# Two plain weight projections of the second block turned into products by blocks

## The chip, the cores and the metric

The kernel runs on one core of a Trainium2 chip, all in 32-bit floats. The metric is the device time of one launch in microseconds (us); three runs of the kernel before gave 4491.0 to 4492.48, with a median of 4491.58.

## The reference

The reference runs a sequence of 1024 tokens with a width of 1024 through two hybrid attention layers (the first block) and then one layer of the second block. Only the end of the second block matters here:

```python
mixed = (jax.nn.sigmoid(gate_a) * y_a + jax.nn.sigmoid(gate_b) * y_b) @ w_out[i]
x = layer_norm_2(DEEPNORM_ALPHA * x + mixed, ln1_g[i], ln1_b[i])

h = causal_dwconv(x @ w_up[i], conv_w[i], conv_b[i])
h_gate, h_val = jnp.split(h, 2, axis=-1)
ffn = (jax.nn.silu(h_gate) * h_val) @ w_down[i]
x = layer_norm_2(DEEPNORM_ALPHA * x + ffn, ln2_g[i], ln2_b[i])

ple = jax.nn.sigmoid(x @ w_ple_gate[i]) * (p[i] @ w_ple[i])
x = layer_norm_2(DEEPNORM_ALPHA * x + ple, ln3_g[i], ln3_b[i])
```

The change is to two 1024x1024 weight products, `@ w_out` (called out2 below) and `x @ w_ple_gate` (the ple gate).

## The kernel before, in words

The program writes one instruction stream for each engine by hand, and semaphores (`wait_ge`, `then_inc`) join them, so each engine runs its instructions in the order of its code and an instruction that waits holds up all that stand behind it. All on-chip data lies in one large tile called arena; all matmul results are in psum. A matmul of 32-bit floats is recorded as two passes on TensorE, and the trace's counts (x256) are counts of passes.

The second block ends in functions named `..._tail`, one for each engine: `pe_tail` (TensorE), `act_tail` (ScalarE), `dve_tail` (VectorE), and the streams of SP and GpSimd. The tokens are two halves of 512 columns (`HALF`), the width is eight tiles of 128 rows (`KD = 8`). On TensorE the order is: eight pairs of the mixing stage (L2773, `product`), out2 (L2739), the first units of the up projection taken plainly (L2727, `plain`), the remaining pairs of the up and down projections (L2773), the small product p @ w_ple (L2845), the ple gate (L2727), and the last normalisation.

A *pair* in this kernel is two output tiles by two runs of tokens that are worked out together by seven block products in place of eight (the scheme of Strassen and Winograd): four sums of weight blocks and four sums of data blocks are made first, and products 1, 6, 7, 4, 5, 2 and 3 are combined into the four output blocks. The mixing, up and down stages of the tail do this with products of 512 columns. The output projection of the first block does it too (`pe_outproj`, L1537), as a chain on 256 columns: each product is four matmuls with 256 columns, products 1, 6 and 7 are copied out of psum by ScalarE (L1675), VectorE adds the others to the copies (L1759), makes the sums of data (L1752) and also the sums of weights (L1741), and the next product of the chain accumulates in psum on top of the one that was copied. out2 and the ple gate are plain: for each half and each output tile, eight matmuls of 512 columns (16 passes).

Between the matmuls of a stage lie the layer normalisations (`layer`, `half`) of the stage before or of the first half of the same stage. Each is a sum of the eight tiles on VectorE (`summed`, L3001), a `mean` matmul (L2749), the subtraction on VectorE (`centre`, L3012), squares on ScalarE (`square`, L2871) that VectorE adds up (`squares`, L3018), a `variance` matmul (L2753), the inverse root on ScalarE (`root`: Ln at L2876 and Exp at L2878, each with a load of its function table), the multiplication by it on VectorE (`scale`, L3028), and gain and bias on ScalarE (`affine`, L2884). Three of them lie beside the two changed stages (`NORMED_IN`): normalisation (0, 0) in the second half of out2, (1, 1) in the first half of the ple gate and (2, 0) in the second. `SUB_SLOTS`, `SQUARE_SLOTS` and `SCALE_SLOTS` say behind which output tile i the centres and squares (i = 1, 2, 3) and the scales and affines (i = 5, 6, 7) stand. The mean of the next one, (0, 1) or (2, 1), follows the last tile.

Weights come as blocks of 512 KB in four buffers (`TAIL_W`), loaded by SP as soon as the block four places earlier is used up (`consumed`). GpSimd does nearly nothing in the tail.

## Time and profile before

| | before |
|---|---|
| median of 3 runs | 4491.58 us (4491.0 to 4492.48) |
| the profiled execution | 4496.65 us |
| its span on the core | 4494.5 us |
| TensorE busy | 4354.1 us, 97% of the span |
| VectorE busy | 2536.8 us, 56% |
| ScalarE busy | 1279.5 us, 28% |
| GpSimd busy | 56.0 us, 1% |
| mean granted clock of TensorE | 0.99 of full speed |
| DMA | 48 GB/s, mean over the span |

The span is what the profiler saw on the core; the time of the execution has 2.15 us around it. The profiled execution was 5.07 us slower than the median of the runs. In rows of the timeline, a number in square brackets is the time for which the engine stood idle before the row, and what it waited for.

### The profile page before, as it was taken

Reading aid. Unit: us, or ns where it says so; the run is one execution under the profiler, and the core shown is the slowest. Engines: PE = TensorE matmul, PEld = TensorE weight load, DVE = VectorE, ACT = ScalarE, POOL = GpSimd, SP = SyncE. Lnnn points to the kernel's source line nnn. Section 1 sums busy time; section 2 is a strip of 40 time slices with the busy share of each in tenths; the row PEclk is TensorE's granted clock in tenths of the full one; section 3 lists DMA queues with packets and bytes.
Section 4 is the critical chain, followed back from the end, with each engine's and each line's share of the span. In section 5 each row is a group of like instructions: output and inputs, shape, how many; then the busy total and the mean of one; then the engine's idle time right before and its main releaser. Section 6 shows DMA issues by size and latency. Waiting matters only on the chain.

```text
span 4494.5 us, 47632 instructions
## 1 busy us (share of the span) xinstructions
PE 4354.1 (97%) x19288; PEld 2491.4 (55%) x19288; DVE 2536.8 (56%) x4202; ACT 1279.5 (28%) x2050; POOL 56.0 (1%) x82
## 2 busy tenths in 40 slices
PE   7999999999998999999999999999999999999997
PEld 3554667886444678844467645555544444444443
DVE  7677556754586567528952314445443555556554
ACT  3004445522025455222023403333200311110024
POOL 1000000000000000000000000000000000000000
PEclk9999999999999999999999999999999999999999
DMA  7212000021120000200110020000122211111112
GB/s 289 75 61 89 1 1 1 2 107 61 47 94 19 1 1 2 84 28 29 38 38 28 20 75 19 20 19 10 38 75 70 69 40 47 47 38 66 47 47 75
DMA packets 50615, 215.57 MB, mean 48 GB/s; under 512 B 5024, under 2 KB 5024, under 8 KB 46816
## 3 DMA queue, kind: packets, MB, share of 16 engines
q1 hardware_dynamic: 36512, 142.62, 9.6%
q0 software_dynamic: 13888, 69.93, 4.1%
q8 instruction: 153, 2.51, 0.2%
q14 instruction: 62, 0.51, 0.0%
HBM read 189.46 MB, written 23.07 MB: 47 GB/s over the span
## 4 chain that ended last, share of the span: by engine, by line
PE 92%; DVE 4%; ACT 2%; DMA 1%; issue 1%; DVEq 0%; SPq 0%; ACTq 0%; POOL 0%; PEld 0%; PEldq 0%
PE psum L2773 21%; PE psum L709 9%; PE psum L1274 7%; PE psum L1312 5%; PE psum L1936 5%; PE psum L1293 5%; PE psum L1537 4%; PE psum L2390 4%; PE psum L399 3%; PE psum L2727 3%; PE psum L2049 3%; PE psum L2039 3%; PE psum L2412 2%; PE psum L2739 2%; PE psum L2076 2%; PE psum L2442 1%
## 5 line engine op out<-in xcount | busy, mean ns | idle before, releaser
L2773 PE MATMUL psum<-arena 128*128 128x512 f32 x2184 | 937.7, 592 | 0.9 <-DVEq L382 0.9
L2773 PEld LDWEIGHTS psum<-arena 128*128 128x128 f32 x2184 | 414.9, 190 | 523.0 <-issue 521.6
L3076 DVE TENSOR_TENSOR arena<-arena,psum 128x512 f32<-128x512 f32 x280 | 192.7, 688 | 405.9 <-PE psum L2773 397.4
L709 PE MATMUL psum<-arena 128*128 128x512 f32 x952 | 410.0, 592 | 0.0
L1274 PE MATMUL psum<-arena 64*128 64x256 f32 (+2 forms) x1584 | 381.9, 441 | 6.8 <-ACT arena L1227 5.8
L709 PEld LDWEIGHTS psum<-arena 128*128 128x128 f32 x952 | 180.9, 190 | 223.8 <-issue 222.4
L1293 PEld LDWEIGHTS psum<-arena 128*128 128x128 f32 x1968 | 229.4, 141 | 125.0 <-issue 102.3
L1347 ACT ACTIVATE arena<-psum,arena 128x1280 f32<-128x1280 f32 (+1 forms) x216 | 265.9, 1241 | 109.6 <-DVE arena L1378 104.6
L1293 PE MATMUL psum<-arena 128*128 128x128 f32 x1968 | 275.5, 275 | 10.8 <-DVE arena L1409 5.8
L1352 ACT ACTIVATE arena<-psum 128x512 f32<-128x512 f32 x294 | 164.8, 597 | 284.6 <-PE psum L1293 284.6
L1312 PE MATMUL psum<-arena 128*64 128x128 f32 x3936 | 238.7, 275 | 4.6 <-DVE arena L1394 2.8
L1312 PEld LDWEIGHTS psum<-arena 128*64 128x64 f32 x3936 | 212.9, 137 | 31.6 <-issue 16.6
L1537 PE MATMUL psum<-arena 128*128 128x256 f32 (+1 forms) x1120 | 222.6, 361 | 6.5 <-ACT arena L1675 4.2
L1936 PE MATMUL psum<-arena 128*128 128x512 f32 x512 | 226.1, 597 | 0.0
L1274 PEld LDWEIGHTS psum<-arena 64*128 64x128 f32 (+1 forms) x1584 | 192.0, 192 | 42.0 <-issue 25.0
L1537 PEld LDWEIGHTS psum<-arena 128*128 128x128 f32 x1120 | 196.7, 191 | 33.2 <-ACT arena L1675 5.4
L1378 DVE TENSOR_REDUCE arena<-psum 128x1 f32<-128x1280 f32 (+1 forms) x120 | 152.2, 1273 | 67.9 <-PE psum L1274 67.8
L2390 PE MATMUL psum<-arena 128*128 128x512 f32 x392 | 175.7, 600 | 0.0
L872 DVE SCALAR_TENSOR_TENSOR arena<-arena 128x1024 f32<-128x1024 f32 (+1 forms) x180 | 172.6, 1014 | 2.1
L2003 DVE TENSOR_SCALAR_CACHE_REDUCE arena<-arena 128x384 f32<-128x384 f32 (+2 forms) x192 | 168.9, 942 | 1.1
L805 DVE TENSOR_TENSOR arena<-arena,psum 128x512 f32<-128x512 f32 x119 | 81.8, 687 | 155.0 <-PE psum L709 145.5
L1394 DVE COPY arena<-psum 128x512 f32<-128x512 f32 x198 | 131.4, 685 | 67.0 <-PE psum L1293 63.6
(314 smaller groups left out, 5453.3 us busy)
## 6 DMA issues: line engine op xcount, KB each, us to landing
arena<-stream SPq DMA_DIRECT2D x228, 512.0 KB, 3.7
arena<-mod_t POOLq DMA_DIRECT2D x32, 512.0 KB, 4.7
arena<-mod_w POOLq DMA_DIRECT2D x4, 2048.0 KB, 16.3
gated<-arena POOLq DMA_DIRECT2D x8, 1024.0 KB, 4.7
arena<-stream SPq DMA_DIRECT2D x6, 1024.0 KB, 10.0
arena<-x SPq DMA_DIRECT2D x4, 1280.0 KB, 15.8
gated<-arena POOLq DMA_DIRECT2D x4, 1280.0 KB, 4.7
arena<-gated SPq DMA_DIRECT2D x1, 5120.0 KB, 15.7
```

What stands on the lines that cost most here:

```text
L709: last = nc.tensor.matmul(ps(PROJECT_BANKS[p], 512), lhsT=lhsT(k), rhs=rhs(k), start=k == 0, stop=k == 3)
L872: last = nc.vector.scalar_tensor_tensor(sb(acc, n), sb(u + i, n), par("dw", off=2 * i + j), sb(acc, n), ALU.mult, ALU.add)
L1274: last = nc.tensor.matmul(ps(score_at(steps[u], s) + c0, n), lhsT=q, rhs=keys, start=True, stop=True)
L1293: last = nc.tensor.transpose(ps(bank(steps[u], g) + i * P, P), sb(P_AT + s * TC + j * P, P), con("ident", P))
L1312: nc.tensor.matmul(ps(BANK7, P, 64 * s, 64 * s + 64), lhsT=sb(at + 64 * s, 64), rhs=sb(PT_AT + (s * nkt + j) * P, P), start=j == 0, stop=j ...
L1347: nc.scalar.activation(sb(P_AT + s * TC, n), ps(score_at(steps[u], s), n), ACT.Exp, bias=sb(MX_AT + s), accum_out=sb(SUM_AT + s)).then_inc ...
L1537: ins = nc.tensor.matmul(ps(out_bank(q, p), h), lhsT=lhsT(k), rhs=rhs(k), start=first and k == 0, stop=k == 3, skip_group_check=not first)
L1936: last = nc.tensor.matmul(ps((b % 2) * 1024 + c0, w), lhsT=sb(W_AT + (g % 2) * 1024 + k * P, P), rhs=x_rhs(k, c0, w), start=k == 0, stop=k ...
L2003: last = nc.vector.tensor_scalar(sb(RELU_AT + mask_at(j) - mask_at(2), w), sb(mask_at(j), w), sb(TRIAL + n), None, ALU.is_ge, ALU.add, acc ...
L2390: last = nc.tensor.matmul(ps(bank, HALF), lhsT=lhsT(k), rhs=rhs(k), start=k == 0, stop=k == 3)
L2773: last = nc.tensor.matmul(ps(pair_bank(j, p), HALF), lhsT=lhsT(k), rhs=rhs(k), start=k == 0, stop=k == nk - 1)
L3076: step(nc.vector.tensor_tensor(out, a, b, op), ev)
```

## The change

out2 and the ple gate are each computed by one chain of seven-product pairs (`chain(0)` and `chain(CHAIN)`). A pair q is two output tiles by one half of the tokens, split into two runs of 256 columns; each chain has eight of them, q = 0 to 7 and q = 8 to 15, the first four for the first half of the tokens. A product is four matmuls of 256 columns, so eight passes. Products 1, 6, 7 and 4 of a pair accumulate in the same bank (`run_bank`), and ScalarE copies the bank out (`copy`) between them, in the same way as in the first block. TensorE's order within a pair is six, five, seven, one of the next pair, four, two of the next pair, three.

The four sums of weights of each pair, 128x512 each, are made by GpSimd (`weight_sums_of`). VectorE makes the four sums of data (`run_sum`, 128x1024) once for each half, adds products to the copies (`read_part`, three for each pair), and writes the outputs (`out2_outputs`, `ple_outputs`). The sigmoid of the ple gate is three instructions for each pair: two of 256 columns and one of 512, the latter (`first_tile_gate`) at the start of the next pair.

The normalisations stay beside the same stages but move to new places (`CENTRED`, `SQUARED`, `SCALED`, by pair): `root` and all eight scales and affines now stand behind pair 7, pair 10 or pair 15, and the variance is a matmul within pair 6, 10 or 14. A weight buffer is used up by product four and by all four sums of weights of its pair. In the chain of the ple gate the mean of (1, 1) stands behind product one of pair 9.

```diff
-    PLAIN = [("out2", v) for v in range(2)] + [("up", v) for v in range(2)]
...
     P1, P2, P6, P7, P4, P5, P3 = range(1, 8)
-    NORMED_IN = {("out2", 1): (0, 0), ("ple", 0): (1, 1), ("ple", 1): (2, 0)}
     SQUARES_BY_DVE = KD * (len(chunks(TC)) + len(chunks(T)) + 5)
-    SUB_SLOTS = {1: range(0, 4), 2: range(4, 8)}
-    SQUARE_SLOTS = {2: range(1, 4), 3: range(4, 8)}
-    SCALE_SLOTS = {5: range(0, 3), 6: range(3, 6), 7: range(6, 8)}
+    QUARTER = 256
+    RUN_PAIRS, CHAIN = KD // 2, KD
+    NORMED_BESIDE = {1: (0, 0), 2: (1, 1), 3: (2, 0)}
+    CENTRED = {4: range(0, 4), 5: range(4, 8), 8: range(0, 4), 9: range(4, 8), 12: range(0, 4), 13: range(4, 8)}
+    SQUARED = {5: range(1, 4), 6: range(4, 8), 9: range(1, 8), 13: range(1, 4), 14: range(4, 8)}
+    SCALED = {7: range(0, 8), 10: range(0, 8), 15: range(0, 8)}
+    C11_READ, C22_READ, C12_READ, C21_READ = 1, 2, 3, 4
...
-        def out2(q, v):
...
-                    t.eng.wait_ge(mixed_done.sem, STORED_PAIRS + i + 1)
...
+        def run_matmuls(q, p, lhsT, rhs, first=False):
+            for k in range(4):
+                ins = nc.tensor.matmul(ps(run_bank(q, p), QUARTER), lhsT=lhsT(k), rhs=rhs(k), start=first and k == 0, stop=k == 3,
+                                       skip_group_check=not first)
+            ins.then_inc(run_product.sem, 1)
...
+                t.eng.wait_ge(run_data_sums.sem, run_data_sums.base + 4 * (q // RUN_PAIRS) + data)
+            if weights:
+                t.eng.wait_ge(run_weight_sums.sem, 4 * q + weights)
...
+        def five(q):
+            summed_for(q, 1, 1)
...
+            run_matmuls(q, 5, lambda k: run_weight_sum(q, 1, k, 1), lambda k: run_data_sum(q, 1, k, 1), first=True)
...
+        def six(q):
+            t.eng.wait_ge(run_copied.sem, run_copied.base + RUN_COPIED[q, 1])
+            summed_for(q, 2, 2)
+            run_matmuls(q, 6, lambda k: run_weight_sum(q, 2, k, 1), lambda k: run_data_sum(q, 2, k, 1))
...
+        def seven(q):
+            t.eng.wait_ge(run_copied.sem, run_copied.base + RUN_COPIED[q, 6])
+            summed_for(q, 3, 3)
+            run_matmuls(q, 7, lambda k: run_weight_sum(q, 3, k, 1), lambda k: run_data_sum(q, 3, k, 1))
...
+        def four(q):
+            t.eng.wait_ge(run_copied.sem, run_copied.base + RUN_COPIED[q, 7])
+            summed_for(q, 4, 0)
+            run_matmuls(q, 4, lambda k: run_weight(q, 1, 1, k, 1), lambda k: run_data_sum(q, 4, k, 1))
...
+        def three(q):
+            summed_for(q, 0, 4)
+            t.eng.wait_ge(run_read.sem, run_read.base + run_read_count(q, C22_READ))
+            run_matmuls(q, 3, lambda k: run_weight_sum(q, 4, k, 1), lambda k: run_data(q, 1, 1, k))
...
+        def chain(first):
+            one(first)
+            five(first)
+            two(first)
+            six(first)
+            one(first + 1)
+            if first:
+                mean(1, 1)
+            seven(first)
+            two(first + 1)
+            four(first)
+            three(first)
+            for q in range(first + 1, first + CHAIN):
+                six(q)
+                if q == CHAIN + 2:
+                    variance(1, 1)
+                five(q)
+                seven(q)
+                if q + 1 < first + CHAIN:
+                    one(q + 1)
+                if q in (RUN_PAIRS, CHAIN + RUN_PAIRS):
+                    mean(*NORMED_BESIDE[q // RUN_PAIRS])
+                if q in (RUN_PAIRS + 2, CHAIN + RUN_PAIRS + 2):
+                    variance(*NORMED_BESIDE[q // RUN_PAIRS])
+                four(q)
+                if q + 1 < first + CHAIN:
+                    two(q + 1)
+                three(q)
 
...
-        for i in range(KD):
-            if i in SUB_SLOTS:
-                for k in SUB_SLOTS[i]:
-                    square(0, 0, k)
-            if i == 4:
-                root(0, 0)
-            for k in SCALE_SLOTS.get(i, ()):
-                affine(0, 0, k)
...
+        def beside(q):
+            norm_of = NORMED_BESIDE.get(q // RUN_PAIRS)
+            for k in CENTRED.get(q, ()):
+                square(*norm_of, k)
+            if q in SCALED:
+                root(*norm_of)
+            for k in SCALED.get(q, ()):
+                affine(*norm_of, k)
+        for q in range(CHAIN):
+            copies(q)
+            beside(q)
...
-            layer, w = NORMED_IN["ple", v]
-            for i in range(KD):
-                r = 2 * KD + v * KD + i
-                if v * KD + i >= 2:
...
-                nc.scalar.activation(sb(PAIR_AT + i % 2 * HALF, HALF), ps(ring(r), HALF), ACT.Sigmoid)\
-                    .then_inc(half_free.sem, 1)
...
-                if i == 4:
-                    root(layer, w)
-                for k in SCALE_SLOTS.get(i, ()):
...
+        def first_tile_gate(q):
+            t.eng.wait_ge(run_read.sem, run_read.base + run_read_count(q, C12_READ))
+            part = sb(run_part_at(q), HALF)
+            nc.scalar.activation(part, part, ACT.Sigmoid).then_inc(run_gate.sem, 1)
+        for q in range(CHAIN, 2 * CHAIN):
+            if q > CHAIN:
+                first_tile_gate(q - 1)
+            copies(q)
+            t.eng.wait_ge(run_product.sem, run_product.base + RUN_PRODUCT[q, 4])
+            nc.scalar.activation(run_part(q, 1, 0), ps(run_bank(q, 4), QUARTER), ACT.Sigmoid).then_inc(run_gate.sem, 1)
+            t.eng.wait_ge(run_read.sem, run_read.base + run_read_count(q, C22_READ))
+            nc.scalar.activation(run_part(q, 1, 1), run_part(q, 1, 1), ACT.Sigmoid).then_inc(run_gate.sem, 1)
+            beside(q)
+        first_tile_gate(2 * CHAIN - 1)
...
-        for v in range(2):
...
-                t.eng.wait_ge(block_used.sem, q + 1)
-                x = ln_tile(0, i, v)
-                step(nc.vector.scalar_tensor_tensor(x, x, ALPHA, ps(ring(q), HALF), ALU.mult, ALU.add), half_free)
-                q += 1
...
-                if v:
-                    centre(0, 0, SUB_SLOTS.get(i, ()))
-                    squares(0, 0, SQUARE_SLOTS.get(i, ()))
-                    scale(0, 0, SCALE_SLOTS.get(i, ()))
...
+        def read_part(q, s, u, p, copied):
+            t.eng.wait_ge(run_product.sem, run_product.base + RUN_PRODUCT[q, p])
+            t.eng.wait_ge(run_copied.sem, run_copied.base + RUN_COPIED[q, copied])
+            out = run_part(q, s, u)
+            step(nc.vector.tensor_tensor(out, out, ps(run_bank(q, p), QUARTER), ALU.add), run_read)
...
+        def out2_outputs(q):
+            v, j = divmod(q, RUN_PAIRS)
...
+            step(nc.vector.scalar_tensor_tensor(x21, x21, ALPHA, ps(run_bank(q, 4), QUARTER), ALU.mult, ALU.add), run_read)
+            nc.vector.scalar_tensor_tensor(x22, x22, ALPHA, run_part(q, 1, 1), ALU.mult, ALU.add)
+            step(nc.vector.scalar_tensor_tensor(x, x, ALPHA, sb(run_part_at(q), HALF), ALU.mult, ALU.add), run_used)
+            t.eng.drain()
+            summed(0, v, 2 * j)
...
+        def ple_outputs(q):
+            v, j = divmod(q - CHAIN, RUN_PAIRS)
...
+            gate = both(run_part_at(q), HALF)
+            t.eng.wait_ge(run_gate.sem, run_gate.base + 3 * (q - CHAIN + 1))
+            step(nc.vector.tensor_tensor(gate, gate, both(PW_AT + (4 * j + v) * HALF, T), ALU.mult))
+            step(nc.vector.scalar_tensor_tensor(both(Z_AT + 2 * j * T + v * HALF, T), both(X_AT + 2 * j * TC + v * HALF, TC), ALPHA, gate,
+                                                ALU.mult, ALU.add), run_used)
+            summed(2, v, 2 * j)
...
+        for q in range(CHAIN):
+            turn = q == RUN_PAIRS - 1
+            read_part(q, 0, 0, 2, 1)
+            if turn:
+                run_sum(1, 1)
+                run_sum(1, 2)
+            read_part(q, 1, 1, 5, 7)
+            if turn:
+                run_sum(1, 3)
+                run_sum(1, 4)
+            beside(q)
+            read_part(q, 0, 1, 3, 6)
+            out2_outputs(q)
...
+        def weight_sums_of(q):
...
+            if 3 <= q < CHAIN or q >= CHAIN + 2:
...
+            a11, a12, a21, a22 = (run_weight(q, s, h) for s in range(2) for h in range(2))
+            old = [run_weight_sum(q, i) for i in range(1, 5)]
+            for out, a, b, op in ((old[0], a21, a22, ALU.add), (old[1], old[0], a11, ALU.subtract), (old[2], a11, a21, ALU.subtract),
+                                  (old[3], a12, old[1], ALU.subtract)):
+                nc.gpsimd.tensor_tensor(out, a, b, op).then_inc(run_weight_sums.sem, 1)
+                t.eng.wait_ge(run_weight_sums.sem, t.next(run_weight_sums))
+        t.eng.wait_ge(mixed_done.sem, STORED_PAIRS + 4)
+        weight_sums_of(0)
```

First, ScalarE's instructions in the ple gate around the end of pair 10, where normalisation (1, 1) gets its root. Before, L2982 is the sigmoid of an output tile, L2876 and L2878 are the root and L2884 the affine:

```order
L2982 ACTIVATE arena<-psum 128x512 x2
L2876 ACT_TABLE_LOAD
L2876 ACTIVATE arena<-psum,arena 128x512
L2878 ACT_TABLE_LOAD
L2878 ACTIVATE arena<-arena 128x512
L2982 ACT_TABLE_LOAD
L2982 ACTIVATE arena<-psum 128x512
L2884 ACTIVATE arena<-arena 128x512 x3
L2982 ACTIVATE arena<-psum 128x512
L2884 ACTIVATE arena<-arena 128x512 x3
L2982 ACTIVATE arena<-psum 128x512
L2884 ACTIVATE arena<-arena 128x512 x2
```

In the changed kernel L3100 is the copy of a product, L3166, L3168 and L3160 are the three sigmoids, L3030 and L3032 the root and L3038 the affine; the first three copies are those of pair 10, and the last three those of pair 11:

```order
L3100 ACTIVATE arena<-psum 128x256 x3
L3166 ACTIVATE arena<-psum 128x256
L3168 ACTIVATE arena<-arena 128x256
L3030 ACT_TABLE_LOAD
L3030 ACTIVATE arena<-psum,arena 128x512
L3032 ACT_TABLE_LOAD
L3032 ACTIVATE arena<-arena 128x512
L3038 ACTIVATE arena<-arena 128x512 x8
L3160 ACT_TABLE_LOAD
L3160 ACTIVATE arena<-arena 128x512
L3100 ACTIVATE arena<-psum 128x256 x3
```

The root, its two table loads and all eight affines now stand in one piece, ahead of the sigmoid of the first tile of pair 10 and ahead of the copies of pair 11; before, a sigmoid stood after the root and after every three affines.

Second, VectorE at the end of out2 and the start of the up projection. Before, L3199 writes an output tile, L3001 is `summed`, L3028 `scale` and L3012 `centre`:

```order
L3199 SCALAR_TENSOR_TENSOR arena<-arena,psum 128x512
L3001 TENSOR_TENSOR arena<-arena 128x512
L3028 TENSOR_TENSOR arena<-arena 128x512 x3
L3199 SCALAR_TENSOR_TENSOR arena<-arena,psum 128x512
L3001 TENSOR_TENSOR arena<-arena 128x512
L3028 TENSOR_TENSOR arena<-arena 128x512 x3
L3199 SCALAR_TENSOR_TENSOR arena<-arena,psum 128x512
L3001 TENSOR_TENSOR arena<-arena 128x512
L3028 TENSOR_TENSOR arena<-arena 128x512 x2
L3012 TENSOR_TENSOR arena<-arena,psum 128x512 x8
```

In the changed kernel L3402 is `read_part`, L3209 `scale`, L3414 to L3416 are the outputs, L3182 `summed` and L3193 `centre`; this is pair 7:

```order
L3182 TENSOR_TENSOR arena<-arena 128x512 x2
L3402 TENSOR_TENSOR arena<-arena,psum 128x256 x2
L3209 TENSOR_TENSOR arena<-arena 128x512 x8
L3402 TENSOR_TENSOR arena<-arena,psum 128x256
L3414 SCALAR_TENSOR_TENSOR arena<-arena,psum 128x256
L3415 SCALAR_TENSOR_TENSOR arena<-arena 128x256
L3416 SCALAR_TENSOR_TENSOR arena<-arena 128x512
L3182 TENSOR_TENSOR arena<-arena 128x512 x2
L3193 TENSOR_TENSOR arena<-arena,psum 128x512 x8
```

All eight scales now stand between two `read_part` of the last pair, and its outputs and sums, on which the mean of (0, 1) rests, come behind them.

Third, ScalarE at the end of the ple gate, where (2, 0) gets its root and (2, 1) follows. Before (names as above, L2871 is the square of (2, 1)):

```order
L2982 ACT_TABLE_LOAD
L2982 ACTIVATE arena<-psum 128x512
L2884 ACTIVATE arena<-arena 128x512 x3
L2982 ACTIVATE arena<-psum 128x512
L2884 ACTIVATE arena<-arena 128x512 x3
L2982 ACTIVATE arena<-psum 128x512
L2884 ACTIVATE arena<-arena 128x512 x2
L2871 ACTIVATE arena<-arena 128x512 x8
```

In the changed kernel, pair 15, with L3025 as the square:

```order
L3100 ACTIVATE arena<-psum 128x256 x2
L3166 ACTIVATE arena<-psum 128x256
L3168 ACTIVATE arena<-arena 128x256
L3030 ACT_TABLE_LOAD
L3030 ACTIVATE arena<-psum,arena 128x512
L3032 ACT_TABLE_LOAD
L3032 ACTIVATE arena<-arena 128x512
L3038 ACTIVATE arena<-arena 128x512 x8
L3160 ACT_TABLE_LOAD
L3160 ACTIVATE arena<-arena 128x512
L3025 ACTIVATE arena<-arena 128x512 x8
```

The last sigmoid (L3160), without which the last output tiles and the sum for the mean of (2, 1) are not made, now stands behind the root, all eight affines and a table load; before, two affines and no table load stood behind the last sigmoid.

## Rows read from the trace of the kernel before

**Rows 1.** The page, part 1: each engine, its busy time and instructions.

```profile
PE 4354.1 (97%) x19288; PEld 2491.4 (55%) x19288; DVE 2536.8 (56%) x4202; ACT 1279.5 (28%) x2050; POOL 56.0 (1%) x82
```

**Rows 2.** Timeline of TensorE, out2 and the up projection: start, duration, count.

```profile
3399.11 21.30 PE L2739 MATMUL psum<-arena 128*128 128x512 f32 x49 [0.85 <-DVE arena L3076]
...
3510.79 3.60 PE L2727 MATMUL psum<-arena 128*128 128x512 f32 x8
3514.23 1.02 PE L2749 MATMUL psum<-arena 128*128 128x512 f32 x2
```

**Rows 3.** Timeline of TensorE, the ple gate and the end.

```profile
4332.18 1.56 PE L2753 MATMUL psum<-arena 128*128 128x512 f32 x2 [2.05 <-DVEq L3021]
4333.53 13.48 PE L2845 MATMUL psum<-arena 128*128 128x512 f32 x28
4346.85 7.03 PE L2727 MATMUL psum<-arena 128*128 128x512 f32 x16
...
4439.66 1.12 PE L2753 MATMUL psum<-arena 128*128 128x512 f32 x2 [0.27 <-DVEq L3021]
...
4464.31 1.12 PE L2749 MATMUL psum<-arena 128*128 128x512 f32 x2 [2.92 <-DVE arena L3001]
```

**Rows 4.** Timeline of TensorE in the first block's chain of pairs.

```profile
1911.35 3.72 PE L1537 MATMUL psum<-arena 128*128 128x256 f32 x16 [0.47 <-ACT arena L1675]
```

**Rows 5.** Timeline of ScalarE in the first block's chain of pairs.

```profile
1846.16 0.39 ACT L1675 ACTIVATE arena<-psum 128x256 f32<-128x256 f32 x1 [5.49 <-PE psum L1537]
...
1858.25 0.39 ACT L1675 ACTIVATE arena<-psum 128x256 f32<-128x256 f32 x1 [5.49 <-PE psum L1537]
```

**Rows 6.** Groups by line and form, VectorE, first block's chain: busy us, mean ns.

```profile
L1759 DVE TENSOR_TENSOR arena<-arena,psum 128x256 f32<-128x256 f32 x24 | 10.1, 421 | 29.1 <-PE psum L1537 17.2 <-ACT arena L1675 10.4 <-issue 1.3
L1752 DVE TENSOR_TENSOR arena<-arena 128x1024 f32<-128x1024 f32 x8 | 9.8, 1225 | 1.9 <-PE psum L1537 1.4 <-PEq L382 0.3
```

**Rows 7.** Timeline of ScalarE, the end of the ple gate and after.

```profile
4440.10 1.28 ACT L2876 ACT_TABLE_LOAD   x1
...
4443.40 0.63 ACT L2878 ACTIVATE arena<-arena 128x512 f32<-128x512 f32 x1
...
4449.02 0.60 ACT L2982 ACTIVATE arena<-psum 128x512 f32<-128x512 f32 x1
...
4480.35 5.75 ACT L2884 ACTIVATE arena<-arena 128x512 f32<-128x512 f32 x8 [0.76 <-DVE arena L3028]
```

**Rows 8.** Timeline of VectorE, the last normalisation.

```profile
4479.63 4.90 DVE L3028 TENSOR_TENSOR arena<-arena 128x512 f32<-128x512 f32 x8 [9.29 <-ACT arena L2878]
```

**Rows 9.** Timeline of VectorE, around the variance in out2.

```profile
3484.18 2.87 DVE L3018 TENSOR_TENSOR arena<-arena 128x512 f32<-128x512 f32 x4
...
3490.26 0.69 DVE L3001 TENSOR_TENSOR arena<-arena 128x512 f32<-128x512 f32 x1
```

**Rows 10.** Groups by line and form, GpSimd, whole span: busy us, mean ns.

```profile
L1044 POOL TENSOR_TENSOR arena<-arena 128x1280 f32<-128x1280 f32 x4 | 9.2, 2312 | 8.8 <-DVE arena L1120 8.8
...
L1044 POOL TENSOR_TENSOR arena<-arena 128x1024 f32<-128x1024 f32 x2 | 3.7, 1883 | 0.0
```

**Rows 11.** The page, part 6: DMA issues, count, size, us to landing.

```profile
arena<-stream SPq DMA_DIRECT2D x228, 512.0 KB, 3.7
```

**Rows 12.** Timeline of TensorE around two waits of earlier stages.

```profile
457.24 7.48 PE L1274 MATMUL psum<-arena 96*128 96x512 f32 x14 [2.57 <-ACT arena L1227]
...
1394.21 4.56 PE L1274 MATMUL psum<-arena 96*128 96x512 f32 x12 [2.14 <-ACT arena L1227]
```

**Rows 13.** Windows: length, PE busy (passes), granted clock, DMA share, GB/s.

```profile
459.00:461.00 2.00, 2.00 (x4) 0.50 0.00 0
...
4334.00:4336.00 2.00, 2.00 (x3) 0.50 0.00 0
4336.00:4338.00 2.00, 2.00 (x6) 0.96 0.00 0
...
1394.00:1397.00 3.00, 2.79 (x8) 1.00 0.02 5
```

More of the change, by code:

```diff
@@ L369, in program @@
     mix_in = event("mix_in", 16)
+    run_weight_sums = event("run_weight_sums")
     p_in = event("p_in", 16)
@@ new lines, in three @@
+        def three(q):
[14 more added lines that the diff above has]
+            three(first)
+            for q in range(first + 1, first + CHAIN):
+                six(q)
[13 more added lines that the diff above has]
+                three(q)
@@ L2851, in pe_tail @@
                 variance(1, 0)
-        for v in range(2):
-            for i in range(KD):
-                r = 2 * KD + v * KD + i
-                bank_free(r)
-                plain(PLAIN_BLOCKS + 2 * len(PAIRS) + v * KD + i, r, lambda k: x_tile(k, v * HALF, HALF), first=i == 0)
-                layer, w = NORMED_IN["ple", v]
-                if i == 0:
-                    mean(layer, w)
-                if i == 4:
-                    variance(layer, w)
+        t.next(half_free, 6)
+        chain(CHAIN)
         mean(2, 1)
```

263 lines of the change are left out of this document (199 added, 64 removed).

## The prediction

> **What bounds the kernel now.** I read the page first: TensorE is busy for 97% of the span [rows 1], so the time is TensorE's passes plus its waits, and the only questions are how many passes the change takes away and how many waits it brings. Then I read TensorE's timeline through the two stages. out2 runs from 3399.11 to 3510.79 with no wait but the 0.85 us at its start [rows 2]. In those 111.68 us lie 260 passes (256 of out2, two of a mean, two of a variance), so a pass of 512 columns takes 0.4295 us. The ple gate runs from 4346.85 with two waits of 0.27 us (one of them shown) to the wait of 2.92 us ahead of the last mean [rows 3]. So both stages are bound by TensorE itself, and everything that stands beside them is hidden. All times below are differences in the profiled execution.
>
> **Passes.** Each stage goes from 256 passes (110.0 us) to eight pairs of seven products. The first block already runs such a chain on 256 columns: the same copy comes at 1846.16 and at 1858.25 [rows 5], so a pair takes 12.09 us and a product 1.73, and eight pairs take 96.7. That is 13.2 us less for each stage, 26.4 in all.
>
> **Work that should stay hidden.** GpSimd's four sums for a pair: 128x1280 takes 2.31 us and 128x1024 takes 1.88 [rows 10]; the line through both gives about 1.0 us for 128x512, the bounds are 0.9 (in proportion) and 1.9. I take 1.0, so 4.1 us for a pair out of 12.09; even 7.5 would fit. The cover is TensorE's pair itself; without it the sums would cost up to 4.1 us a pair. A weight buffer is free after product four and the next load into it is needed by product one five products later, 8.6 us, against 3.7 us from issue to landing [rows 11]; SP has nothing else to issue there. VectorE's reads of products (0.42 us each [rows 6]) and ScalarE's copies (0.39 [rows 5]) fit into a pair as they do in the first block. Each of these is costed at nothing, except at the places below, where a long piece of normalisation stands ahead of them.
>
> **Waits in out2.** I follow each engine's queue in the new order with the durations of before.
> - Start: the last read of psum ends some 0.8 us after the last mixing matmul, which is the 0.85 of [rows 2]. Behind it stand a data sum of 1.23 us [rows 6], for which product five waits 0.3, and two products of the mixing of the same size, for which product two waits 0.75. Together 1.1 in place of 0.85: +0.3.
> - Variance of (0, 0): VectorE's four last adds (2.87 us [rows 9]) stand behind a read that waits for the copy of product seven of pair 6. Semaphore 0.2, copy 0.4, read 0.45, adds 2.87, semaphore 0.2: 4.1 us after that product, with only product one of pair 7 (1.73) to cover it: +2.4.
> - Product four of pair 7 has no product of a next pair ahead of it and waits for its copy. The first block's chain ends the same way, with 0.47 us idle [rows 4]; a row's modelled end lies 0.16 behind the next start where nothing waits (3510.79 + 3.60 against 3514.23 [rows 2]), which is lost too: +0.6.
> - Up projection, first unit: it needs the first affine of (0, 0). Counted from the end of product seven of pair 7: copy at 0.6, root with its two table loads 3.9 (4440.10 to 4444.03 [rows 7]), scale 0.6, affine 0.7 to 0.8: 6.0, against 4.1 at which TensorE is done with four and three: +1.9.
> - Mean of (0, 1): on VectorE the eight scales (4.90 us [rows 8]) now stand ahead of the last read and the outputs. Root at 4.5, scales to 9.4, then the read and two outputs of 256 columns (0.45 each, after the read's 0.42) and one of 512 (0.72), a drain, two sums of 0.72 [rows 9]: 13.0. TensorE comes to it at 6.0 plus eight passes (3.4): +3.6. In before it waited for nothing at 3514.23 [rows 2].
>
> Sum of out2: -13.2 + 0.3 + 2.4 + 0.6 + 1.9 + 3.6 = -4.4 us.
>
> **Waits in the ple gate.**
> - Squares of (1, 1) around pairs 9 and 10: by the same arithmetic 0.3 and 0.5 us, together +0.9 with rounding (0 to 2).
> - Product seven of pair 11 waits for the copy of product six, and on ScalarE that copy now stands behind the whole piece of (1, 1). From the end of product four of pair 10: two sigmoids to 1.0, root 3.9, scale 0.6, eight affines 5.75 [rows 7], table load 1.28, sigmoid 0.6, copy 0.4: 13.6. TensorE has two, three, six and five to do: 6.9. So +6.7.
> - Variance of (2, 0) in pair 14, as in out2: +2.4. Product four of pair 15: +0.6. The two waits of 0.27 are gone: -0.5.
> - The end. From the end of product seven of pair 15: copy and product four to 2.4, two sigmoids to 3.3, root to 7.2, scale 0.6, eight affines to 13.6, table load and last sigmoid to 15.5, two output instructions over 1024 columns (1.23 each, as the data sum) and two sums to 19.5. TensorE is done at 4.1 and waits 15.4, where it waited 2.92 [rows 3]: +12.5. What is late next is the whole last normalisation; nothing lies beside it, so all of it counts.
>
> Sum of the ple gate: -13.2 + 0.9 + 6.7 + 2.4 + 0.6 - 0.5 + 12.5 = +9.4 us.
>
> **The clock.** A wait costs more than itself when TensorE comes back at half speed. After 2.05 us of idling at 4332.18 the granted clock was 0.50 (1.2 GHz) until about 4336 [rows 3, 13]; from 4332.18 to 4346.85 there are 30 passes, which at full clock take 12.9 us and took 14.7, so that wait cost 1.8 us on top. After 2.57 us at 457.24 it fell too, after 2.14 us at 1394.21 it did not [rows 12, 13]. So I charge 1.8 for the wait of 6.7 and for that of 3.6, half of it for each of the two of 2.4, and 0.9 for the last mean, whose two passes run at half clock: 1.8 + 1.8 + 1.8 + 0.9 = 6.3. The bounds are 0 and 8.1.
>
> Sum: -4.4 + 9.4 + 6.3 = +11.3 us. The profiled execution of 4496.65 (span 4494.5, and 2.15 around it) would become 4508; it lay 5.07 above the median, so on the median of 4491.58 this is 4503.
>
> **Rivals.**
> 1. *The clock stays up* through these waits, as it did after 2.14 us [rows 12, 13]. Then the change costs 5.0 us: 4496.6, which is not slower by what can be told. The deciding point: the forecast needs 4.0 us of clock loss to be over 9.0. Against it: 2.05 and 2.57 did bring it down, and 3.6 and 6.7 are longer.
> 2. *GpSimd and VectorE hold each other up.* Both now read arena at the same time, which no row of before shows: GpSimd's few sums ran beside other things. The places are VectorE's adds ahead of the variances in pairs 6, 10 and 14. If each instruction excludes the other engine's, an add waits for up to one sum of 1.0 us; GpSimd is busy a third of the time, and at three places of four to seven adds, part of them with slack, this makes about +2.4, so 4505; with sums of 1.9 it could be +12. The Trainium skill (SBUF — State Buffer, "Who interferes with whom") says that a VectorE instruction with two inputs in SBUF contends with a GpSimd instruction that reads SBUF, and that the one that comes second blocks fully. By that rule this rival holds; no run here shows it yet.
> 3. *ScalarE's pieces delay nobody*: the copies of pair 11 and the last sigmoid pass the affines in some way. That takes back 6.7, 12.5 and 2.7 of clock: 4481. Against it stands the order of the rows on ScalarE, which runs its queue in order.
> 4. *GpSimd becomes the bound.* From 3.0 us for a sum on (12.09 / 4) the chain would run at its pace; at 3.5 that is 2 us a pair, over 30 in all: 4535. The rows [rows 10] are far from it.
>
> **How the numbers follow.** Forecast 0.45, rival 1 0.25, rival 2 0.23, rival 3 0.05, rival 4 0.02. A difference of 0.2%, 9.0 us, is about what a measurement of this kernel can tell from none; the bound lies at 4500.6. Of the forecast and rival 2 a fifth falls under it, when the clock loss is smaller; rival 1 is the same but for a little; rival 3 is faster. So slower 0.57, same 0.37, faster 0.06. The likeliest case alone runs from 4499 to 4506; the range takes in rival 1 with the small waits at nothing (4493) and rival 2 with slow sums in part (4511).
>
> **What the profile after would show.** TensorE: same copies 12.1 us apart in quiet pairs; a wait of about 6 to 7 us ahead of product seven of pair 11 put down to a copy; 15 us ahead of the last mean; 2.4 ahead of the variances in pairs 6 and 14; 3.6 ahead of the mean of (0, 1). GpSimd: sums of about 1.0 us. The prediction is wrong if the wait of pair 11 or the last one is half of that, if pairs without a normalisation take more than 12.5 us, or if the granted clock stays at 1.00 after waits over 2.5 us.

## The result and the profile after

The changed kernel takes 4516.34 us (median of 4 runs, 4513.0 to 4520.98) against 4491.9 for the kernel before in the same runs: ratio 1.005, interval 1.0038 to 1.0063. It is slower, as forecast, but by about 24 us where 11 were worked out, and outside the stated range. The profiled execution is the fastest of the four, 4513.0 with a span of 4510.9; against the profiled execution of before that is 16.35 us more.

The page of the changed kernel, part 1:

```profile
PE 4336.0 (96%) x19672; PEld 2564.3 (57%) x19672; DVE 2607.0 (58%) x4258; ACT 1297.5 (29%) x2106; POOL 153.7 (3%) x146
```

TensorE is busy for 18 us less than in [rows 1], and GpSimd for 98 us more. The windows of the changed kernel by stretch (length, PE busy and passes, granted clock, DMA share, GB/s): the chain of out2 with the plain units of the up projection, the stages between, and the ple gate with all behind it.

```profile
3396.98:3564.84 167.86, 159.08 (x585) 0.99 0.24 79
3564.84:4342.55 777.71, 774.72 (x1805) 1.00 0.14 47
4342.55:4510.90 168.35, 117.12 (x475) 0.85 0.18 63
```

The same three stretches of the kernel before (the first starts at 3399.11 less its wait of 0.85):

```profile
3398.26:3567.44 169.18, 168.33 (x392) 1.00 0.26 78
3567.44:4346.85 779.41, 776.42 (x1805) 1.00 0.14 47
4346.85:4494.50 147.65, 125.07 (x283) 0.93 0.22 71
```

The first stretch is 1.3 us shorter, the middle one 1.7 shorter (behind the wait of 2.05 us of [rows 3], which both kernels have, the clock did not fall this time), the last one 20.7 us longer; the chain of out2 also starts 1.3 us earlier. The forecast was -1.7 for the first (with its share of the clock) and +13 for the last. TensorE's timeline in the first stretch of the changed kernel:

```profile
3396.98 1.89 PE L2812 MATMUL psum<-arena 128*128 128x256 f32 x8
...
3458.72 1.13 PE L2917 MATMUL psum<-arena 128*128 128x512 f32 x2 [0.70 <-DVE arena L3182]
...
3487.25 1.13 PE L2921 MATMUL psum<-arena 128*128 128x512 f32 x2 [3.23 <-DVEq L3202]
...
3499.21 3.72 PE L2812 MATMUL psum<-arena 128*128 128x256 f32 x16 [0.47 <-ACT arena L3100]
3504.89 5.37 PE L2806 MATMUL psum<-arena 128*128 128x512 f32 x8 [1.96 <-ACT arena L3038]
3511.52 1.13 PE L2917 MATMUL psum<-arena 128*128 128x512 f32 x2 [1.26 <-DVE arena L3182]
```

The waits follow the forecast's list: variance of (0, 0) 3.23 (2.4 forecast), product four of pair 7 0.47, first affine 1.96 (1.9), mean of (0, 1) 1.26 (3.6; TensorE came to it later, since the eight passes ahead of it took 5.37 us where the same eight take 3.67 in e1 below; the granted clock was 0.72 from 3504 to 3508). New is 0.70 ahead of the mean of (0, 0). In the ple gate:

```profile
4373.81 1.12 PE L2921 MATMUL psum<-arena 128*128 128x512 f32 x2 [0.88 <-DVEq L3202]
...
4399.24 17.88 PE L2812 MATMUL psum<-arena 128*128 128x256 f32 x72 [10.50 <-ACT arena L3100]
...
4447.26 1.53 PE L2921 MATMUL psum<-arena 128*128 128x512 f32 x2 [4.75 <-DVEq L3202]
...
4480.18 2.08 PE L2917 MATMUL psum<-arena 128*128 128x512 f32 x2 [15.55 <-DVE arena L3182]
```

The last mean waits 15.55, where 15.4 was worked out. But product seven of pair 11 waits 10.50 (6.7 forecast) and the variance of (2, 0) 4.75 (2.4). VectorE just before the first of these:

```profile
4381.55 0.42 DVE L3402 TENSOR_TENSOR arena<-arena,psum 128x256 f32<-128x256 f32 x1
4386.61 9.21 DVE L3209 TENSOR_TENSOR arena<-arena 128x512 f32<-128x512 f32 x8 [4.64 <-ACT arena L3032]
4395.74 0.86 DVE L3402 TENSOR_TENSOR arena<-arena,psum 128x256 f32<-128x256 f32 x2
```

The eight scales of (1, 1) take 9.21 us, where the eight scales of the last normalisation took 4.90 in [rows 8]; the reads of psum around them keep their 0.42 each. GpSimd at that place:

```profile
4386.97 6.49 POOL L3624 TENSOR_TENSOR arena<-arena 128x512 f32<-128x512 f32 x4 [6.73 <-DMA arena<-stream]
```

The four sums of a pair start 0.36 us after the scales. Through out2 the same shows in VectorE's groups (busy us, mean ns): `summed` (L3182), with two inputs in arena, went from 0.69 to 1.25 us on the mean, and `read_part` (L3402), with one input in psum, takes what it took in [rows 6], also where it lies beside one of GpSimd's sums (15 of its 48 in the two stages).

```profile
L3182 DVE TENSOR_TENSOR arena<-arena 128x512 f32<-128x512 f32 x14 | 17.6, 1254 | 1.0
...
L3402 DVE TENSOR_TENSOR arena<-arena,psum 128x256 f32<-128x256 f32 x24 | 10.1, 420 | 31.2 <-PE psum L2812 24.8 <-ACT arena L3100 5.9
```

### The profile page after: what moved, and what is told of

It is laid out like the page before. It is cut to its first block, busy times and chain, and to the rows that moved or that the text cites. A ratio compares the mean times of both kernels' runs of the same rounds, so it can differ in the third digit from the quotient of the medians.

```text
span 4510.9 us, 48765 instructions
## 1 busy us (share of the span) xinstructions
PE 4336.0 (96%) x19672; PEld 2564.3 (57%) x19672; DVE 2607.0 (58%) x4258; ACT 1297.5 (29%) x2106; POOL 153.7 (3%) x146
## 4 chain that ended last, share of the span: by engine, by line
PE 91%; DVE 5%; ACT 2%; DMA 1%; issue 1%; DVEq 0%; SPq 0%; ACTq 0%; POOL 0%; PEld 0%; PEldq 0%
PE psum L2941 21%; PE psum L713 9%; PE psum L1278 7%; PE psum L1316 5%; PE psum L1940 5%; PE psum L1297 5%; PE psum L1541 4%; PE psum L2394 4%; PE psum L403 3%; PE psum L2812 3%; PE psum L2053 3%; PE psum L2043 3%; PE psum L2416 2%; PE psum L2080 2%; PE psum L2446 1%; PE psum L722 1%
## 5 line engine op out<-in xcount | busy, mean ns | idle before, releaser
L2941 PEld LDWEIGHTS psum<-arena 128*128 128x128 f32 x2184 | 414.9, 190 | 523.0 <-issue 521.6
L3257 DVE TENSOR_TENSOR arena<-arena,psum 128x512 f32<-128x512 f32 x280 | 192.3, 687 | 406.2 <-PE psum L2941 397.7
L713 PEld LDWEIGHTS psum<-arena 128*128 128x128 f32 x952 | 180.9, 190 | 223.8 <-issue 222.2
L1297 PEld LDWEIGHTS psum<-arena 128*128 128x128 f32 x1968 | 229.4, 141 | 124.8 <-issue 102.3
L1541 PEld LDWEIGHTS psum<-arena 128*128 128x128 f32 x1120 | 196.7, 191 | 33.2 <-ACT arena L1679 5.4
L2812 PE MATMUL psum<-arena 128*128 128x256 f32 x896 | 199.9, 384 | 12.6 <-ACT arena L3100 11.4
L2812 PEld LDWEIGHTS psum<-arena 128*128 128x128 f32 x896 | 172.2, 193 | 42.8 <-ACT arena L3100 12.9
```

The source lines that it names most:

```text
L713: last = nc.tensor.matmul(ps(PROJECT_BANKS[p], 512), lhsT=lhsT(k), rhs=rhs(k), start=k == 0, stop=k == 3)
L1297: last = nc.tensor.transpose(ps(bank(steps[u], g) + i * P, P), sb(P_AT + s * TC + j * P, P), con("ident", P))
L1541: ins = nc.tensor.matmul(ps(out_bank(q, p), h), lhsT=lhsT(k), rhs=rhs(k), start=first and k == 0, stop=k == 3, skip_group_check=not first)
L2812: ins = nc.tensor.matmul(ps(run_bank(q, p), QUARTER), lhsT=lhsT(k), rhs=rhs(k), start=first and k == 0, stop=k == 3, skip_group_check=not ...
L2941: last = nc.tensor.matmul(ps(pair_bank(j, p), HALF), lhsT=lhsT(k), rhs=rhs(k), start=k == 0, stop=k == nk - 1)
L3257: step(nc.vector.tensor_tensor(out, a, b, op), ev)
```

## The experiments

Theory A: GpSimd and VectorE exclude each other while both read arena, and this lengthens VectorE's pieces at the places where TensorE waits for them. Theory B, the rival: the longer instructions are hidden, and the excess over the forecast is clock or run-to-run spread. A third reading, that TensorE waits for GpSimd's sums themselves, is ruled out by the trace: from 3390 us on no wait of TensorE in the changed kernel is put down to GpSimd. A second question is whether the forecast's own mechanism, the pieces of normalisation standing in one block in the queues, is right.

All results, each beside the kernel before on the same chip; the last two columns are the first and the last stretch of the profiled execution, as in the windows above (before: 169.2 and 147.6).

| kernel | median us | before | difference | ratio, interval | out2 stretch | ple stretch |
|---|---|---|---|---|---|---|
| changed | 4516.34 | 4491.9 | +24.4 | 1.0038 to 1.0063 | 167.9 | 168.4 |
| changed, again | 4520.24 | 4496.42 | +23.8 | 1.0033 to 1.0061 | 172.8 | 169.0 |
| e1, sums of 16 columns | 4503.49 | 4496.09 | +7.4 | 1.001 to 1.0028 | 166.9 | 158.8 |
| e5, GpSimd only writes | 4503.26 | 4496.42 | +6.8 | 1.0003 to 1.0021 | 166.9 | 158.8 |
| e2, sums by VectorE | 4513.31 | 4496.09 | +17.2 | 1.003 to 1.0057 | 170.3 | 169.5 |
| e3, ple pieces apart | 4503.38 | 4496.09 | +7.3 | 1.0013 to 1.0031 | 172.5 | 156.0 |
| e4, out2 only | 4499.36 | 4496.09 | +3.3 | 0.9992 to 1.0011 | 172.4 | 147.7 |
| e6, apart everywhere | 4494.72 | 4496.42 | -1.7 | 0.9989 to 1.0007 | 163.4 | 151.9 |
| e7, apart, sums by VectorE | 4486.67 | 4496.42 | -9.8 | 0.9968 to 0.9987 | 160.1 | 149.6 |
| e9, e7 with two orders changed | 4486.72 | 4494.68 | -8.0 | 0.9972 to 0.999 | 159.7 | 148.2 |

### e1: GpSimd's sums over 16 of 512 columns

```diff
+                out, a, b = (y[:, 0:16] for y in (out, a, b))
                 nc.gpsimd.tensor_tensor(out, a, b, op).then_inc(run_weight_sums.sem, 1)
```

> This kernel is the changed one, but each of GpSimd's 64 sums of weights covers 16 of its 512 columns, so most of the weight sums are left out; orders and waits are the same. Theory A (GpSimd and VectorE exclude each other while both read arena with two inputs): VectorE's scales of (1, 1) go from 9.2 us for eight back to 4.9, its sums of 128x512 back to 0.69 each, the wait ahead of product seven of pair 11 from 10.5 to about 6.7, that ahead of the variance of (2, 0) from 4.75 to about 2.4, and the time to about 4503 us (4498 to 4507). Theory B (VectorE's longer instructions are hidden, and the excess over the forecast comes from the clock or from run to run): the two waits shrink by less than 1 us and the time stays at 4513 to 4521.

Measured: +7.4 us. TensorE's timeline in the ple gate:

```profile
4389.06 17.39 PE L2812 MATMUL psum<-arena 128*128 128x256 f32 x72 [6.60 <-ACT arena L3100]
...
4433.75 1.12 PE L2921 MATMUL psum<-arena 128*128 128x512 f32 x2 [2.26 <-DVEq L3202]
...
4464.97 2.07 PE L2917 MATMUL psum<-arena 128*128 128x512 f32 x2 [15.55 <-DVE arena L3182]
```

With GpSimd's long reads gone, the waits are those that the forecast had worked out from before's durations alone: 6.60 (6.7), 2.26 (2.4), 15.55 (15.4). The eight scales of (1, 1) took 5.00 us. Theory B falls.

### e5: GpSimd writes the same area and reads nothing

```diff
-                nc.gpsimd.tensor_tensor(out, a, b, op).then_inc(run_weight_sums.sem, 1)
+                nc.gpsimd.memset(out, 0.0).then_inc(run_weight_sums.sem, 1)
```

> GpSimd writes zeros over the whole 128x512 of each sum of weights and reads nothing, so the weight sums are left out; orders and waits are those of the changed kernel. Theory A1 (VectorE is held up by GpSimd's reads of arena): VectorE's two-input instructions stay at 0.69 us for 512 columns although GpSimd is busy beside them; scales of (1, 1) 4.9 us for eight, wait ahead of product seven of pair 11 about 6.6, and 7 to 9 us over the kernel before, as with the sums of 16 columns. Theory A2 (any GpSimd instruction on arena holds VectorE up): the scales take over 7 us for eight while GpSimd writes, the wait stays over 8, and the time is 14 us or more over before.

Measured: +6.8 us, the same as e1 and just under the 7 to 9 expected. VectorE's scales of (1, 1), and GpSimd beside them:

```profile
4385.87 4.91 DVE L3209 TENSOR_TENSOR arena<-arena 128x512 f32<-128x512 f32 x8 [7.12 <-ACT arena L3032]
```

```profile
4386.16 2.27 POOL L3624 MEMSET arena<- 128x512 f32 x4 [10.56 <-DMA arena<-stream]
```

The scales keep 4.91 us for eight while GpSimd writes for 2.27 us in the midst of them. So it is GpSimd's reading of arena, or the adding that goes with it, that holds VectorE up (theory A1), not its being busy or its writing.

### e2: the sums of weights by VectorE

```diff
             if turn:
                 run_sum(1, 3)
                 run_sum(1, 4)
+            if q + 1 < CHAIN:
+                weight_sums_of(q + 1)
             beside(q)
```

The same stands in the loop of the ple gate, pair 0's sums stand ahead of the last mixing pair and pair 8's ahead of `run_sum(2, 1)`; the body of `weight_sums_of` is GpSimd's, with `nc.vector`.

> The 64 sums of weights move from GpSimd to VectorE, those of the next pair ahead of the normalisation piece of each pair (pair 0's ahead of the last mixing pair). Theory A: VectorE's instructions are at their short durations everywhere, but four adds of 0.7 us (2.9 in all) now stand ahead of the last adds of the variances in pairs 6, 10 and 14, so these waits grow to about 5 us each, the wait ahead of product seven of pair 11 stays at about 6.7; time about 4511 (4504 to 4518), with a run-to-run spread as small as that of the kernel before. Theory B: VectorE has 2.9 us more for each pair and nothing is given back, so 4520 or more.

Measured: +17.2 us, 7 less than with GpSimd. The waits in question, of the variances of pairs 6, 10 and 14 and of product seven of pair 11:

```profile
3484.95 2.08 PE L2921 MATMUL psum<-arena 128*128 128x512 f32 x2 [5.15 <-DVEq L3202]
...
4375.71 1.12 PE L2921 MATMUL psum<-arena 128*128 128x512 f32 x2 [2.83 <-DVEq L3202]
...
4398.94 18.44 PE L2812 MATMUL psum<-arena 128*128 128x256 f32 x72 [6.61 <-ACT arena L3100]
...
4448.79 2.08 PE L2921 MATMUL psum<-arena 128*128 128x512 f32 x2 [6.36 <-DVEq L3202]
```

Nothing is lengthened (6.61 at pair 11), but four adds ahead of the variances put 2.9 us on each wait in out2 and pair 10, and 4.1 on that of pair 14. Standing ahead of the adds, the sums are in TensorE's way on VectorE too.

### e3: the pieces of normalisation in the ple gate taken apart

```diff
-    SCALED = {7: range(0, 8), 10: range(0, 8), 15: range(0, 8)}
+    SCALED = {7: range(0, 8)}
+    ROOTS = {10: (1, 1), 14: (2, 0)}
...
-            copies(q)
+            if q - 1 in ROOTS:
+                copy(q, 6)
+                for k in range(5):
+                    affine(*ROOTS[q - 1], k)
+                copy(q, 7)
+                for k in range(5, KD):
+                    affine(*ROOTS[q - 1], k)
+                if q + 1 < 2 * CHAIN:
+                    copy(q + 1, 1)
+            else:
+                copies(q)
...
             beside(q)
+            if q in ROOTS:
+                root(*ROOTS[q])
...
             read_part(q, 0, 1, 3, 6)
+            if q in ROOTS:
+                scale(*ROOTS[q], range(KD))
```

In pairs 11 and 15 VectorE also reads product five ahead of the outputs of the pair before, and in pair 11 it makes all four data sums behind these.

> Only the ple gate is altered. The roots stand behind pairs 10 and 14, the eight affines stand between the copies of the next pair, behind the sigmoid of the first tile and the copy of product six, and VectorE's scales stand behind the last read of the pair. Queue theory (the waits ahead of product seven of pair 11 and ahead of the last mean come from the one piece on ScalarE): the first falls from 10.5 us to under 1.5, the last from 15.5 to about 8, up to 4 us of this come back as waits for the reads and data sums of VectorE, and the time is about 4499 (4494 to 4505). Rival (VectorE under GpSimd's sums sets these waits, whatever ScalarE's order): both shrink by less than a third and the time stays over 4508.

Measured: +7.3 us, so 16 to 17 less than the changed kernel. TensorE in the ple gate:

```profile
4396.03 8.83 PE L2813 MATMUL psum<-arena 128*128 128x256 f32 x32 [2.56 <-ACT arena L3039]
4405.89 3.69 PE L2813 MATMUL psum<-arena 128*128 128x256 f32 x16 [1.03 <-issue]
...
4446.21 2.07 PE L2922 MATMUL psum<-arena 128*128 128x512 f32 x2 [4.75 <-DVEq L3215]
...
4471.71 2.08 PE L2918 MATMUL psum<-arena 128*128 128x512 f32 x2 [5.96 <-DVE arena L3195]
```

The last mean waits 5.96 in place of 15.55, and product seven of pair 11 no longer waits. In place of its 10.50 there are 6.45 behind it: 2.56 ahead of product one of pair 12, which needs the affines, 1.03 and 1.12 in that pair, and 1.74 ahead of the mean of (2, 0); up to 4 were expected. The forecast's mechanism holds: what TensorE waited for was the order on ScalarE, lengthened by VectorE. The ple stretch is 12.4 us shorter, although GpSimd still lengthens the scales (9.20 us for eight) and the adds (the variance of pair 14 waits 4.75 as before).

### e4: only out2 changed

The ple gate's four engines run the lines of the kernel before, with the counts of semaphores adapted; out2 is as in the changed kernel.

> Only out2 is a chain of pairs; the ple gate is plain, as in the kernel before. From the two profiles the stretch from the end of the mixing products to the first pair of the up projection takes 167.7 us where it took 169.2, so if the stages are independent the time is 1 to 3 us under that of the kernel before: about 4490 (4486 to 4494). If out2 leaves something behind that costs time later (loads that come later, the clock), it is over 4495.

Measured: a ratio of 1.0002, no difference that can be told, where 1 to 3 us less than before were expected: that gain was missed. The ple stretch is that of before (147.7), so out2 leaves nothing behind there, and most of the loss is the ple gate's. The expectation took out2 at the 167.9 of the changed kernel's first execution; with the same code it takes 172.4 in this one, 3.2 more than before. TensorE in it:

```profile
3482.93 1.12 PE L2927 MATMUL psum<-arena 128*128 128x512 f32 x2 [3.19 <-DVEq L3217]
...
3508.89 2.08 PE L2923 MATMUL psum<-arena 128*128 128x512 f32 x2 [2.97 <-DVE arena L3197]
3510.76 12.60 PE L2812 MATMUL psum<-arena 128*128 128x512 f32 x24
```

### The changed kernel again, and the clock

> The changed kernel itself beside the others on one chip, since the kernel before took 4491.9 us in one place and 4496.1 in another. Theory A expects +22 us against before (18 to 26), the wait ahead of product seven of pair 11 between 8 and 11 us depending on where GpSimd's sums fall, and a spread of several us from run to run.

Measured: +23.8 us, with 10.48 at pair 11, 4.75 at pair 14 and 15.55 at the end, as in the first profile. What differs is the out2 stretch, 172.8 in place of 167.9. This execution at the variance of (0, 0), and the windows behind it:

```profile
3487.55 2.08 PE L2921 MATMUL psum<-arena 128*128 128x512 f32 x2 [3.19 <-DVEq L3202]
```

```profile
3487.00:3490.00 3.00, 2.45 (x4) 0.50 0.00 0
3490.00:3493.00 3.00, 3.00 (x9) 0.50 0.00 0
```

The first profile of the same kernel, where the same wait was 3.23:

```profile
3487.00:3490.00 3.00, 2.75 (x11) 1.00 0.02 5
3490.00:3493.00 3.00, 3.00 (x16) 1.00 0.62 160
```

After nearly equal waits TensorE's granted clock was 0.50 in one execution and 1.00 in the other. So part of the spread of the changed kernel (4513.0 to 4521.35 over all its runs) is the clock's. That the other short waits act in the same way is likely, but was not followed run by run.

### e6 and e7: the pieces apart in both stages, and the sums moved

```diff
+    ROOTS = {6: (0, 0), 10: (1, 1), 14: (2, 0)}
...
             beside(q)
+            if q in ROOTS:
+                scale(0, 0, range(0, 2))
             read_part(q, 0, 1, 3, 6)
             out2_outputs(q)
+            if q in ROOTS:
+                scale(0, 0, range(2, KD))
...
-                if q in (RUN_PAIRS + 2, CHAIN + RUN_PAIRS + 2):
-                    variance(*NORMED_BESIDE[q // RUN_PAIRS])
                 four(q)
+                if q in (RUN_PAIRS + 2, CHAIN + RUN_PAIRS + 2):
+                    variance(*NORMED_BESIDE[q // RUN_PAIRS])
```

ScalarE's root of (0, 0) stands behind pair 6 and its affines between the copies of pair 7, as in e3.

> The pieces of normalisation are taken apart in out2 too (root of (0, 0) behind pair 6, its scales and affines spread over pairs 6 and 7), and the three variances stand one product later; the sums of weights stay on GpSimd. Queue theory: against the kernel that took apart only the ple gate (7 to 10 us over before) the mean of (0, 1) waits under 1.5 us where it waited 2.97, the first unit of the up projection 0 where it waited 1.96, the variances of pairs 6 and 14 about 1.5 and 3; with one or two fewer stretches at half clock that is 8 to 11 us less: -3 to +1 us against before. Rival (the waits only move, since VectorE and ScalarE have the same work behind them): less than 3 us are gained.

Measured: -1.7 us, within what can be told. The rows that answer to the expectation:

```profile
3488.04 1.13 PE L2922 MATMUL psum<-arena 128*128 128x512 f32 x2 [1.56 <-DVEq L3227]
...
3499.82 5.41 PE L2813 MATMUL psum<-arena 128*128 128x256 f32 x16 [2.02 <-ACT arena L3101]
...
3508.82 1.12 PE L2918 MATMUL psum<-arena 128*128 128x512 f32 x2 [0.16 <-DVE arena L3207]
...
4391.31 12.49 PE L2813 MATMUL psum<-arena 128*128 128x256 f32 x48 [3.38 <-ACT arena L3039]
...
4440.45 1.13 PE L2922 MATMUL psum<-arena 128*128 128x512 f32 x2 [3.04 <-DVEq L3227]
```

The mean of (0, 1) waits 0.16 and the variances 1.56 and 3.04, as expected; 2.02 at product four of pair 7 is new, where the copy now stands behind affines. The 3.38 stand ahead of product one of pair 12, which needs the affines of (1, 1). With e7's sums on VectorE, behind the adds in pairs 6 and 14:

```diff
+            more = (q + 1) % CHAIN != 0
+            if more and q not in (RUN_PAIRS + 2, CHAIN + RUN_PAIRS + 2):
+                weight_sums_of(q + 1)
             for do, slots in ((centre, CENTRED), (squares, SQUARED), (scale, SCALED)):
                 if q in slots:
                     do(*norm_of, slots[q])
+            if q in (RUN_PAIRS + 2, CHAIN + RUN_PAIRS + 2):
+                weight_sums_of(q + 1)
```

> The same as the kernel with pieces apart everywhere, but the sums of weights are VectorE's, behind the adds of the variances in pairs 6 and 14 and ahead of the piece elsewhere. Theory A: no VectorE instruction is lengthened; the variances of pairs 6 and 14 wait about 0.7 each, that of pair 10 about 1; against GpSimd's sums this gives 2 to 4 us, so -6 to -2 us against before. If VectorE's queue is full, the waits move to products three and to the outputs and it is slower than with GpSimd.

Measured: -9.8 us, the first version that beats the kernel before (ratio 0.9978), and by more than the 2 to 6 expected.

```profile
3484.96 1.13 PE L2922 MATMUL psum<-arena 128*128 128x512 f32 x2 [0.52 <-DVEq L3227]
...
3496.81 3.72 PE L2813 MATMUL psum<-arena 128*128 128x256 f32 x16 [2.09 <-ACT arena L3101]
...
4397.51 8.60 PE L2813 MATMUL psum<-arena 128*128 128x256 f32 x32 [4.84 <-DVE arena L3408]
...
4434.63 1.12 PE L2922 MATMUL psum<-arena 128*128 128x512 f32 x2 [1.73 <-DVEq L3227]
...
4454.88 2.07 PE L2918 MATMUL psum<-arena 128*128 128x512 f32 x2 [5.96 <-DVE arena L3207]
```

The variance of pair 6 waits 0.52, that of pair 14 1.73 (0.7 expected). 4.84 us stand behind pair 11, ahead of product six of pair 12: VectorE's four data sums come ahead of the weight sums that this product needs. e2 and e7 make the same sums on the same engine; that they stand behind the adds, and the pieces apart, is worth 27 us between them.

### e9: two more orders changed

Against e7:

```diff
-                for k in range(2, 5):
-                    affine(0, 0, k)
                 copy(q, 7)
-                for k in range(5, KD):
+                for k in range(2, KD):
                     affine(0, 0, k)
...
-            if more and q not in (RUN_PAIRS + 2, CHAIN + RUN_PAIRS + 2):
+            if more and q not in (RUN_PAIRS + 2, CHAIN + RUN_PAIRS - 1, CHAIN + RUN_PAIRS + 2):
...
             read_part(q, 0, 0, 2, 1)
+            if turn:
+                weight_sums_of(q + 1)
```

> The kernel with pieces apart and VectorE's weight sums, with two waits of its trace taken up: the weight sums of pair 12 stand ahead of the data sums of the second half (TensorE waited 4.84 us for them behind pair 11), and the copy of product seven of pair 7 stands ahead of the affines 2 to 4 (2.09 us). Queue theory: these waits fall to about 1 and 0.5, and a stretch at half clock behind the first goes with it; 5 to 7 us less than that kernel, so -17 to -14 us against the kernel before. Rival (VectorE's queue as a whole is late there, so the wait only changes its name): under 2 us are gained.

Measured: 4486.72, as e7; the expectation was missed.

```profile
3490.50 1.99 PE L2813 MATMUL psum<-arena 128*128 128x256 f32 x8 [0.47 <-ACT arena L3101]
3493.48 1.97 PE L2813 MATMUL psum<-arena 128*128 128x256 f32 x8 [0.99 <-DVE arena L3445]
...
4392.24 8.83 PE L2813 MATMUL psum<-arena 128*128 128x256 f32 x32 [2.96 <-issue]
```

Product four of pair 7 waits 0.47 as expected, but then product three waits 0.99 for VectorE's read. Behind pair 11 the wait is 2.96, and it is product six of pair 12 again, which also needs the second data sum; VectorE makes the four of them now behind the weight sums, and the second ends about 4392.1:

```profile
4389.65 5.00 DVE L3439 TENSOR_TENSOR arena<-arena 128x1024 f32<-128x1024 f32 x4
```

The rival was right here: VectorE is late as a whole at these two places, and the wait changes its name. By the stretches 1.8 us were gained, which the run times do not show.

## Why the prediction was wrong, step by step

- **Passes: right.** In e1, 256 passes of 256 columns lie between 3397.43 and 3452.79, 0.2163 us each or 12.1 us for a pair, as forecast.
- **Waits from the order of the queues: right in place, and in size to within 0.7 us.** Without GpSimd's reads (e1) they are 2.25, 0.47, 1.96 and 2.97 in out2 (forecast 2.4, 0.6 with the drain, 1.9, 3.6) and 6.60, 2.26, 0.47 and 15.55 in the ple gate (6.7, 2.4, 0.6, 15.4). The small waits at pairs 9 and 10, put at 0.9, are nothing there. e3 and e6 show by moving the pieces that the order is their cause.
- **The clock: mis-sized, and not steady.** 6.3 us were charged; e1, which holds the other terms of the forecast, came out at +7.4 in place of +11.3 (by its stretches -2.3 and +11.1, where -1.7 and +13.0 were worked out). 0.9 of the difference are the small waits; that the rest is the clock is argued and not shown. In e1 the wait of 2.97 cost nothing more (24 passes behind it took 10.46 us), while in e4 the same wait was followed by 12.60 for 24. One of the forecast's own signs of being wrong came too: behind the wait of 3.23 in the first profile the granted clock stayed at 1.00.
- **GpSimd's sums "costed at nothing": the step that failed.** That they fit into a pair's 12.09 us was true, and the estimate of 1.0 us for a sum was near (1.09 at the least, 1.27 where VectorE stood still, 1.53 on the mean). But their reading holds VectorE up, and VectorE's pieces were on TensorE's path. From e1 and e5 to the changed kernel that is 16 to 17 us by the medians: about 10 of it in the ple stretch (3.9 at pair 11, 2.5 at pair 14, 0.9 at pair 10, and some 2 in which TensorE ran slower behind these waits, as in the 48 passes behind the variance of pair 14: 11.85 us against 10.52), and 1 in out2 in the first profile, 6 in the second.
- **Rival 2 named this and mis-sized it**: +2.4, with up to +12 for slow sums. It spread the sums evenly and let a third of VectorE's adds meet one. The sums are not spread: they start when the weights land or a buffer comes free, and at pair 11 all four fell into the eight scales, which rival 2 did not even name. The Trainium skill (SBUF — State Buffer, "Who interferes with whom") says that the second to issue blocks for the whole instruction, and that a GpSimd instruction that only writes does not contend. The traces agree with both: a scale comes every 0.61 us back to back and every 1.68 where it meets a sum, 1.07 more, which is most of the sum's 1.27, and e5 showed no hold-up. The affines, each behind its scale, show the 1.68:

```profile
4387.34 0.81 ACT L3038 ACTIVATE arena<-arena 128x512 f32<-128x512 f32 x1 [0.83 <-DVE arena L3209]
4389.02 0.81 ACT L3038 ACTIVATE arena<-arena 128x512 f32<-128x512 f32 x1 [0.87 <-DVE arena L3209]
```

What stays open is what decides whether the clock falls after a wait of 2 to 3.3 us, and with it some 5 us of the spread. The kernel before has a spread of its own (its 26 runs beside e5 lie at 4491.0 to 4493.3 and at 4495.9 to 4497.6), whose cause was not tried.

## What to carry to other kernels

An engine with spare time is not free: before work is given to GpSimd, look at which of VectorE's instructions read two operands from the same memory at that time, and price each meeting at nearly the whole of the other's instruction (1.07 of 1.27 us here), at the places where the work really falls, not on the mean. When a tight chain replaces a loose loop, the pieces that were spread over the loop must be spread again: here, in the ple gate, a root, its table loads and eight affines in one block made about 19 us of new waits in e1 (6.60, and 15.55 in place of 2.92), more than the 13.2 that the products by blocks saved; taken apart, in e3, about 9.5. Short waits can have a second price in TensorE's clock, and it is not the same in every execution.
